# Two extra whole-word products inside the second up-projection round of three feed-forward halves

## What is computed

```python
def rms_norm(x, g):
    y = xf * lax.rsqrt(jnp.mean(xf * xf, axis=-1, keepdims=True) + NORM_EPS)
    return (y * g).astype(x.dtype)

def swiglu(x, w_gu, w_down):
    gate, up = jnp.split(x @ w_gu, 2, axis=-1)
    return (jax.nn.silu(gate) * up) @ w_down

x = x + 0.5 * swiglu(rms_norm(x, p['norm_ffn1']), p['ffn1_w_gu'], p['ffn1_w_down'])
# retention, RWKV-7 and their gated merge: x = x + merged @ w_out
x = x + 0.5 * swiglu(rms_norm(x, p['norm_ffn2']), p['ffn2_w_gu'], p['ffn2_w_down'])
```

## Time and profile before

| what | us |
|---|---|
| median of 3 runs | 2853.31 |
| the runs | 2839.84, 2853.31, 2854.24 |
| span of the profiled execution | 2831.2 |
| its own time, not recorded apart: the span and what lies around it; by the lowest run | 2839.84 |
| TensorE busy | 2803.7 |
| VectorE busy | 1563.9 |
| ScalarE busy | 1116.5 |
| GpSimd busy | 107.1 |

### The profile page before, as it was taken

The page is one execution under the profiler, slowest core; times in us unless marked ns, Lnnn a source line. Parts: engine busy times, 40 slices in busy tenths (PEclk is TensorE's granted clock), DMA queues, the critical chain, the costliest instruction groups (busy, mean ns, idle before and its releaser), DMA issues.

```text
span 2831.2 us, 57289 instructions
## 1 busy us (share of the span) xinstructions
PE 2803.7 (99%) x24662; PEld 2731.8 (96%) x24662; DVE 1563.9 (55%) x1679; ACT 1116.5 (39%) x1121; POOL 107.1 (4%) x144
## 2 busy tenths in 40 slices
PE   9999999999999999999999999999999999999998
PEld 8999999999999999898998999999999999999998
DVE  6544444454566576775865655466544544444454
ACT  5333333333344453544534644233433333333333
POOL 0000000000000002011020010000000000000000
PEclk9999999999999999999999999999999999999999
DMA  5444454444556543635436544555444445444454
GB/s 209 168 169 162 165 179 171 173 168 157 172 189 235 199 174 123 235 135 201 163 134 240 188 145 164 190 201 202 164 165 176 159 164 180 170 174 164 159 173 146
DMA packets 85460, 495.80 MB, mean 175 GB/s; under 512 B 10320, under 2 KB 10496, under 8 KB 44096
## 3 DMA queue, kind: packets, MB, share of 16 engines
q1 hardware_dynamic: 71424, 444.14, 44.7%
q0 software_dynamic: 9280, 32.72, 3.2%
q10 hardware_dynamic: 4608, 16.78, 1.5%
HBM read 462.80 MB, written 30.80 MB: 174 GB/s over the span
## 4 chain that ended last, share of the span: by engine, by line
PE 89%; DVE 5%; DMA 3%; ACT 2%; issue 1%; SPq 0%; ACTq 0%; DVEq 0%; POOLq 0%
PE psum L546 28%; PE psum L547 27%; PE psum L548 27%; DVE sb_w_lo L1507 1%; DMA out_ret_s<-sb_s_ret 1%; DVE sb_w_lo L1513 1%; ACT sb_w_hi L1086 1%; PE psum L894 1%; DMA sb_raw<-in_w_wo 1%; DMA sb_s_ret<-in_s_ret 1%; PE psum L710 1%; DVE sb_s_ret L1884 0%; ACT sb_w_hi L1095 0%; DMA sb_raw<-in_gu 0%; PE psum L907 0%
## 5 line engine op out<-in xcount | busy, mean ns | idle before, releaser
L546 PE MATMUL psum<-sb_h,sb_w_hi 128*128 128x288 f32 x4384 | 1303.7, 297 | 4.6 <-DVE sb_w_lo L1507 2.2
L547 PE MATMUL psum<-sb_h,sb_w_hi 128*128 128x288 f32 x4384 | 1278.8, 292 | 0.0
L548 PE MATMUL psum<-sb_h,sb_w_lo 128*128 128x288 f32 x4384 | 1275.1, 291 | 0.0
L1513 DVE TENSOR_TENSOR sb_w_lo<-sb_raw,sb_w_hi 128x2048 fp32r<-128x2048 f32 (+1 forms) x348 | 712.3, 2047 | 697.1 <-ACT sb_w_hi L1086 696.4
L1086 ACT ACTIVATE sb_w_hi<-sb_raw 128x2048 fp32r<-128x2048 f32 (+1 forms) x349 | 600.1, 1719 | 1176.9 <-PE psum L548 1140.2
L546 PEld LDWEIGHTS psum<-sb_h,sb_w_hi 128*128 128x128 f32 x4384 | 823.5, 188 | 29.0 <-issue 19.0
L548 PEld LDWEIGHTS psum<-sb_h,sb_w_lo 128*128 128x128 f32 x4384 | 825.4, 188 | 0.0
L547 PEld LDWEIGHTS psum<-sb_h,sb_w_hi 128*128 128x128 f32 x4384 | 824.0, 188 | 1.3 <-issue 1.0
L546 PE MATMUL psum<-sb_g,sb_w_hi 128*128 128x288 f32 x1408 | 412.5, 293 | 0.0
L547 PE MATMUL psum<-sb_g,sb_w_hi 128*128 128x288 f32 x1408 | 409.7, 291 | 0.0
L548 PE MATMUL psum<-sb_g,sb_w_lo 128*128 128x288 f32 x1408 | 408.3, 290 | 0.0
(11 more groups left out here) (380 smaller groups left out, 2385.8 us busy)
## 6 DMA issues: line engine op xcount, KB each, us to landing
sb_raw<-in_gu SPq DMA_DIRECT2D x175, 1024.0 KB, 4.8
sb_raw<-in_down SPq DMA_DIRECT2D x128, 704.0 KB, 4.1
sb_raw<-in_w_mix SPq DMA_DIRECT2D x72, 1024.0 KB, 5.1
sb_raw<-in_w_gates SPq DMA_DIRECT2D x32, 1024.0 KB, 5.4
sb_s_ret<-in_s_ret POOLq DMA_DIRECT2D x32, 512.0 KB, 8.1
out_ret_s<-sb_s_ret ACTq DMA_DIRECT2D x32, 512.0 KB, 5.3
sb_raw<-in_w_ro SPq DMA_DIRECT2D x16, 1024.0 KB, 4.8
sb_raw<-in_w_out SPq DMA_DIRECT2D x16, 1024.0 KB, 4.8
```

The lines of the kernel that those rows point to most:

```text
L546: pe.matmul(out, wh, xh, start=start, stop=False)
L547: pe.matmul(out, wh, xl, start=False, stop=False)
L548: return pe.matmul(out, wl, xh, start=False, stop=stop)
L1513: dve.tensor_tensor(w_lo[:, slot, 0:cols], raw[:, slot, 0:cols], w_hi[:, slot, 0:cols].bitcast(F32), ALU.subtract).then_inc(lo_made, 2)
```

## The change

A function `break_in` is added. It runs two whole-word products of `mean_w` with `sum_sq` into bank 4, waits for nothing and increments nothing; its result is not used. It is called at unit 8 of the second pair of round 1 (the second round) of the halves (n, f) = (0, 0), (0, 1) and (1, 1), not of (1, 0). Round 1 is written out beside round 0 in all four halves, and the hardware loop begins at round 2.

```diff
--- before.py
+++ after.py
@@ -600,15 +600,25 @@
                     norm(r)
                 return run
 
+            def break_in():
+
+                for k in range(2):
+                    pe.matmul(psum[:, 4, 0:T], mean_w[:, :], sum_sq[:, k, :], start=(k == 0), stop=(k == 1))
+
             def feed(n):
                 for f in range(2):
                     up_ph, down_ph = (*ffn[n][f][0], 4, 2), (*ffn[n][f][1], 8, 2)
 
                     def up(i):
                         enter = is_first(i) and f == 0
+                        second = isinstance(i, int) and i == 1 and (n, f) != (1, 0)
                         pair(i, up_ph, 0, 0, 2, KT, h_hi, h_lo, ready=gained_by(2 * n) if enter else None, halves=enter and n == 0)
-                        pair(i, up_ph, 2, 1, 2, KT, h_hi, h_lo, between=mean(2 * n) if enter else None, unit=8 if n else 16)
-                    loop(pe, HT // 2, up)
+                        pair(i, up_ph, 2, 1, 2, KT, h_hi, h_lo, between=break_in if second else mean(2 * n) if enter else None,
+                             unit=8 if n or second else 16)
+                    up(0)
+                    up(1)
+                    with pe.Fori(2, HT // 2) as i:
+                        up(i)
                     done = (2 * n + f) * (HT // 2)
 
                     def down(i):
```

## The result

The changed kernel takes 2887.91 us (median of 6 runs, 2875.3 to 2892.97) against 2853.77 for the kernel before: ratio 1.0141, 95% interval 1.0107 to 1.0175. One of the six runs of the kernel before stands far apart at 3956.92 us and is not in the ratio. The changed kernel is slower, by more than the range allowed. The profiled execution has a span of 2890.2 us where that of before had 2831.2, so 59.0 us came in between the two traces.

A forecast was written before the change was run, and what follows sets the result against it. TensorE, busy 99% at full clock, was taken to bound the kernel. The lowest run, 2839.84 us, plus 3.4 us for three calls of two products gave 2843.2 us, slow halves being reset by the restart; range 2834 to 2862.

The forecast's parts named there:

- What bounds the kernel: Whole span: TensorE busy 99% at full clock sets the length; ScalarE and VectorE follow it, so added TensorE work is uncovered.
- A restart chooses anew: Behind the products: a half entered slow leaves that rhythm after 312 matmuls, losing 0.7 us in place of 7.0.
- The price of the products: At the three calls of the two added products: 1.13 us each, 3.4 us in all, bounds 2.6 to 5.8.
- The entry to the loop: First half at 37.87: entering the loop cost 0.10 us and now comes a round later; taken as 0 over all halves.
- Restarts behind whole-word products ended at the short one in all the feeds that the trace shows: Feeds' mean products: streams behind them ran at 128.9 ns, taken as support for the same behind the new products.
- the restart lands in a slower rhythm: Rival, behind the new products: 131.1 ns gives 2862 us, 136 ns in all three halves 2904; chance 0.11.
- The spread of the runs: Two of three earlier runs, 13.5 and 14.4 us longer: explained by two halves at 131.1 ns, 13.9 us.
- 8.6 us "around the span": Profiled execution of the kernel before: taken as the lowest run's kind, 2839.84 us, with 8.6 us outside its 2831.2 us span.
- The Trainium skill's rule: Warm matmul gap of columns / 2.4 plus 2.5 ns, 122.5 for 288 columns; products then only add themselves.
- cost only: Rival, whole kernel: run spread comes from elsewhere, so the median only rises by 3.4 us to 2856.7; chance 0.25.
- shorter rhythm: Rival, behind the products: a pace under 128.9 ns; at 127 ns 16 us gained, about 2827 us; chance 0.07.
- the loop's entry behind the products: Rival, at round 2: entering the loop interrupts again and may undo the choice; runs stay mixed, 2843 to 2857; chance 0.08.

The follow-up runs named there:

- e1: The change with round 1 still written out but without its two whole-word products: 2857.39 us, ratio 1.0032 to the kernel before.
- e6_drained_two: The change with its two products at unit 16, TensorE first waiting until its last matmul has ended: 2841.19 us, ratio 0.9983 to the kernel before.
- e4: The change with its two products at unit 16 of the second pair, not unit 8: 2893.73 us, ratio 1.0188 to the kernel before.
- e5: The change plus four whole-word products at the same unit two rounds later, rounds 0 to 3 written out: 2855.82 us, one run.
- e9: The change plus one whole-word product at the same unit two rounds later, rounds 0 to 3 written out: 2892.26 us, one run.
- e11: The kernel before with two whole-word products ahead of both second halves, no round written out: 2877.13 us, one run.
- e8: The change with three whole-word products in place of two at the same places: 2840.96 us, 8 runs.
- e14: The change with a TensorE pause at unit 16 until its last matmul has ended, and no products: 2837.81 us, one run.
- e15: The change with a TensorE pause at unit 16 and no products, timed over 12 runs: 2840.95 us, ratio 0.9971 to the kernel before.
- e12_three_everywhere: The kernel before with three products ahead of both second halves and at the start of the first half's round 1: 2837.86 us, ratio 0.9964.
- e10: The kernel before with three whole-word products ahead of both second halves, no round written out: 2838.93 us, ratio 0.9967.

## Why the prediction was wrong

The forecast was 2843.2 us, range 2834 to 2862; measured were 2887.91. Point by point:

*What bounds the kernel* held. TensorE's pace in the feeds is the time, ScalarE and VectorE follow it, and nothing that they do changed.

*That the pace has several rhythms which last* held and is the main thing. "A restart chooses anew" held with one exception: a single product hands on what it meets.

*The price of the products* was 1.13 us each; measured are 54.97 - 54.08 - 0.13 + (0.35 - 0.13) = 0.98. The stall ahead of the earlier trace rows had added 0.1 to my figure. Half of the 1.72 us of four products seemed to confirm it, but the eight passes there hold seven full distances of 0.24 us, and two products hold three.

*The entry to the loop* was read wrongly from the earlier trace rows, as e1 shows: it costs nothing, and the step at 37.87 belongs to the start of round 1. Nothing in the sum hung on it.

*The step that failed* is the sentence "Restarts behind whole-word products ended at the short one in all the feeds that the trace shows". It rested on two cases, and I counted both as the same as the new one. One was two products behind a stall, the other four products. The first was no support for a long stretch at all: 48 matmuls behind it comes the step of the earlier trace rows, where the 383 us begin, and in two of the 17 traces the same two products led to 135.5 ns. The new one was two products behind a running stream, which no row showed. The experiments show the difference in each direction: with a pause two give 128.9 ns in the three halves of e6_drained_two, four and three give it without one, and two without one give 135.6 in all fourteen halves of five traces (the change, e4, e5, e9, e11), each time behind a stream at 128.9. What I had priced as the rival, "the restart lands in a slower rhythm", is what happened, in the form that the prediction had at 2904 us. I had 20.3 us for a half at 136 ns from a window of 36 matmuls; over a whole half it is 135.6 ns and 19.1 us. The rest of the distance from 2904 is in the price of the products, in the base of the sum, of which the next point speaks, and in the two low runs that pull the median down. Its chance of 0.11 was too low for a place at which, in my own words, no trace had a restart.

*The spread of the runs* I read as two halves at 131.1 ns, 13.9 us. The traces show single halves at 135.6 ns behind a plain stall in e1, e6, e8, e14 and e15, always the first feed's second half, and 21 us for a whole one. These are five of the fourteen traces in which that entrance is a plain stall; the second feed's second half came in at 128.9 ns in the same fourteen. What the runs near 2875 us of the kernel before are, no trace shows. The 8.6 us "around the span" were wrong with it: a run of the changed kernel with a span of 2890.2 took 2892.0, so 1.8 us lie around. The profiled execution of before was one of about 2833 us, at the bottom of its spread and 20 us under its median. Sums against it must not be set against the median without a word on the group.

*The Trainium skill's rule* ("TensorE: Matmul & The Clock Gate", section "Back-to-back issue gap") was applied too widely. The section gives columns / 2.4 plus 2.5 ns, by which I estimated 122.5 ns, for an isolated matmul; for streams of weight load plus matmul it gives about 81 ns at 128 columns and 131 ns at 512. The long stretches of all these traces, 288 columns wide, are at 128.9, 131.1 and 135.6 ns for one form, and 132.3 on other tiles, so 122.5 was not met in any of them. The formula has no term for what ran before, but the section does not claim that for streams; "with no memory" was my own reading. Had it held, the change would have cost its 3 us alone.

*The other rivals:* cost only is out, since the stream behind the products changed; no shorter rhythm than 128.9 lasted in any half of a trace; the loop's entry behind the products undid nothing.

Shown by the runs: that the rhythm is chosen at interruptions, that it lasts, that two products behind a running stream at 128.9 ns bring 135.6, one passes on what it meets, three and four bring 128.9, and that the time of the interruption alone does not decide. Only argued: that all slow runs of the kernel before are badly drawn halves, which the vanished upper group of e12_three_everywhere supports. Open: why two passes more or fewer make the difference, what two products do to a stream at 135.6, what the two runs of the change near 2875 us are, and whether a pause alone is safe.

## What to carry to other kernels

In a stream of back-to-back matmuls, divide stretch by count in several windows before trusting a pace: a busy share of 99% hides 5%. Where the paces differ for one form, look at the last interruption before each, and treat an interruption with another length or another state ahead of it as a new case, not as a seen one. When a kernel's runs fall into groups, find out which group the profile is of, and time a candidate with enough runs to see the groups.

## What was not expected of the hardware

The same three matmuls per product, on the same tiles and at the same granted clock of 1.00, have steady paces of 128.9, 131.1 and 135.6 ns; the first and the last were held over a whole half of 3168 matmuls, 131.1 over 2976 (e10). Two whole-word products in a running stream (four passes, 0.98 us in all) led from 128.9 to 135.6 ns in all fourteen traced halves; six passes and eight lead back, and two passes hand on what they find. A wait of 0.32 us on VectorE, the same to the hundredth, was followed by 128.9 ns in one trace and 135.6 in another.

The views round to 0.01 us; the starts in the packed traces have whole ns and show the rhythm from the first interval on. Where the entrance of the first feed's second half is a plain stall, the first matmul is followed by the second after 205 to 209 ns in the nine traces that went on at 128.9, and after 214 or 215 in the five that went on at 135.6. Behind full-width whole-word products in a running stream it is 343 to 349 ns ahead of 128.9 and 353 or 354 ahead of 135.6. What sets this interval, no run shows.
